# First block of a two-block network: attention bias added by VectorE from a stored band, a value group between the first heads, first branch's product beside the last heads

## The reference

```python
mod = (silu(c) @ w_mod + b_mod)                  # 6 x 1024, one row
h = rms_norm(x, norm_mix) * (1 + scale_m) + shift_m
qa, ka, va, xr, yr, qc, kc, vc, g_logits = split(h @ w_in)
# q and k are normalised by head of 64; 8 heads of branch a (window 128, a sink
# each), 8 heads of branch c; bias by distance q - k from a table per head
s = q @ k.T / 8 + bias[q - k]                    # causal
p = softmax(s)                                   # with the sink in branch a
o_a, o_c = p @ v
o_b = rg_lru(conv(xr)) * gelu(yr)
merged = g0 * (o_a @ wb[:512]) + g1 * (o_b @ wb[512:1536]) + g2 * (o_c @ wb[1536:])
x = x + gate_m * (merged @ w_out)                # g = sigmoid(g_logits)
```

## Time and profile before

| | us |
|---|---|
| median of 3 runs (2408.05 to 2409.7) | 2408.58 |
| the profiled execution | 2410.9 |
| its span, first to last instruction | 2409.2 |
| first dense matmul starts | 49.95 |
| end of the first value group | 170.5 |
| first g group starts | 208.93 |
| first branch_b group starts | 328.3 |
| w_out starts | 393.78 |

### The profile page before, as it was taken

How to read it: one execution, slowest core, us unless ns; L and a number is a source line. 1 busy time by engine, 2 the same in 40 slices (tenths; PEclk the granted TensorE clock), 3 DMA queues, 4 the chain that set the end, 5 groups by cost and what they waited for, 6 DMA issues and landing times.

```text
span 2409.2 us, 35095 instructions
## 1 busy us (share of the span) xinstructions
PE 2258.7 (94%) x14043; PEld 2032.7 (84%) x14043; DVE 1762.6 (73%) x1924; ACT 1324.5 (55%) x1277; POOL 53.0 (2%) x112
## 2 busy tenths in 40 slices
PE   7989998998998889999888699999999999999997
PEld 6987888998998879999888688888888888888886
DVE  5765756787598555547865388988888888888885
ACT  2563432663454444435344376767777776777674
POOL 5000000000000000000000000000000000000000
PEclk7997999999999999999999799999999999999998
DMA  8543754565743526665443299999999899999992
GB/s 260 175 153 115 226 162 145 154 186 178 205 154 108 158 78 187 182 181 165 127 140 125 71 375 329 370 342 354 369 332 373 321 374 338 366 326 366 332 382 108
DMA packets 414056, 565.70 MB, mean 235 GB/s; under 512 B 16330, under 2 KB 267444, under 8 KB 413904
## 3 DMA queue, kind: packets, MB, share of 16 engines
q1 hardware_dynamic: 410160, 556.31, 68.2%
q0 software_dynamic: 3456, 6.13, 1.2%
q10 hardware_dynamic: 288, 1.05, 0.1%
HBM read 562.37 MB, written 1.08 MB: 234 GB/s over the span
## 4 chain that ended last, share of the span: by engine, by line
PE 80%; DVE 9%; ACT 4%; issue 2%; DMA 0%; ACTq 0%; DVEq 0%
PE pair L1017 57%; PE misc L1017 13%; DVE arena L1882 2%; DVE wlo L1539 2%; PE misc L1412 1%; PE pair L1423 1%; ACT whi L594 1%; PE misc L1447 1%; PE misc L1196 1%; PE misc L1195 1%; PE misc L1080 1%; DVE rt L1564 1%; PE misc L1324 0%; DVE opl L1557 0%; DVE opf L1597 0%
## 5 line engine op out<-in xcount | busy, mean ns | idle before, releaser
L2078 DVE TENSOR_TENSOR wlo<-raw,whi 128x2048 fp32r<-128x2048 f32 x338 | 770.1, 2290 | 124.1 <-ACT whi L948 122.8
L948 ACT CAST whi<-raw 128x2048 fp32r<-128x2048 f32 x338 | 647.2, 1918 | 202.4 <-PE pair L1017 101.0
L1017 PE MATMUL pair<-hh,whi 128*128 128x256 f32 x1840 | 533.2, 290 | 28.0 <-DVE hl L1557 19.6
L1539 DVE TENSOR_TENSOR wlo<-raw,whi 128x2048 fp32r<-128x2048 f32 (+1 forms) x170 | 384.6, 2264 | 197.7 <-ACT whi L594 197.1
L1017 PE MATMUL pair<-hl,whi 128*128 128x256 f32 x1840 | 527.8, 287 | 0.0
L1017 PE MATMUL pair<-hh,wlo 128*128 128x256 f32 x1840 | 527.6, 287 | 0.0
L1017 PE MATMUL pair<-whi,oph 128*128 128x512 f32 (+1 forms) x1024 | 394.1, 385 | 5.3 <-DVE wlo L2078 3.6
L1017 PEld LDWEIGHTS pair<-hh,whi 128*128 128x128 f32 x1840 | 361.1, 196 | 33.7 <-issue 32.7
L1017 PE MATMUL pair<-wlo,oph 128*128 128x512 f32 (+1 forms) x1024 | 386.6, 378 | 0.0
L1017 PE MATMUL pair<-whi,opl 128*128 128x512 f32 (+1 forms) x1024 | 385.9, 377 | 0.0
L1017 PEld LDWEIGHTS pair<-hl,whi 128*128 128x128 f32 x1840 | 361.0, 196 | 0.3
(11 more groups left out here) (408 smaller groups left out, 2552.7 us busy)
## 6 DMA issues: line engine op xcount, KB each, us to landing
raw<-in_moe_w_gate_dram SPq DMA_DIRECT2D x114, 1024.0 KB, 7.3
raw<-in_moe_w_up_dram SPq DMA_DIRECT2D x112, 1024.0 KB, 7.3
raw<-in_moe_w_down_dram SPq DMA_DIRECT2D x112, 1024.0 KB, 6.9
raw<-in_w_in_dram SPq DMA_DIRECT2D x38, 1024.0 KB, 5.4
raw<-in_w_mod_dram SPq DMA_DIRECT2D x24, 1024.0 KB, 6.8
raw<-in_w_up_dram SPq DMA_DIRECT2D x44, 512.0 KB, 5.0
raw<-in_w_xkv_dram SPq DMA_DIRECT2D x16, 1024.0 KB, 5.6
raw<-in_ffn_w_gate_dram SPq DMA_DIRECT2D x22, 512.0 KB, 3.9
```

What stands on the lines that cost most here:

```text
L948: act.copy(whi[:, q, :], raw[:, r, :]).then_inc(sem("hi_ready"), 1)
L1017: ins = pe.matmul(out_, lhs, rhs, start=start and i == 0, stop=stop and i == 2)
L1539: dve.tensor_tensor(wlo[:, i_ % SPLIT, 0:size], raw[:, raw_of(n), 0:size], whi[:, i_ % SPLIT, 0:size].bitcast(F32), ALU.subtract).then_inc ...
L2078: dve.tensor_tensor(wlo[:, q, :], raw[:, r, :], whi[:, q, :].bitcast(F32), ALU.subtract).then_inc(sem("lo_ready"), 1)
```

## The change

- Bias: GpSimd stores each head's bias row 128 times, 384 wide, in DRAM (`bias_bands`), and loads it for a head with a row step of 383, so that partition q holds the bias of query q. `peak` becomes two `tensor_tensor_reduce` instructions: scores from PSUM plus band, written to SBUF, with the maximum as a second result. The bias matmuls and the flipped identity go. The exponentials read SBUF.
- Order at the start of attention: spreads and scores of the first heads come before the second value group, and VectorE's reciprocal no longer stands behind the splits of g slots.
- Branches: branch_a (half a slot) runs beside each of the last four heads, after branch_b; four groups branch_c of half a slot follow the heads; w_out's first group waits chunk by chunk.
- Start: of the first eight modulator slots PE takes 0, 2, 5 and 7, by products with one stationary column and 256 moving ones, a copy by ScalarE and a turn; slot 7 is loaded after xr's first slot. The tables for norms of q and k are made after the vector loads.
- Two places only change how a semaphore is named (feed-forward taps; `bc_done`).

```diff
-    modulator(8)
+    modulator(7)
     for j in range(4):
         dense("xr", w_in, [(XR + j * 256, 256)], "act")
+        modulator(j == 0)
...
         modulator(j == 0)
+        dense("branch_a", wb, [(j * 256, 256)], "dve", kchunks=4)
     for j in range(4):
-        parts = [(rows(wb, 0, 4), 0, 4, j * 256, 256, 0), (rows(wb, 12, 4), 4, 4, j * 256, 256, 0)]
-        groups.append(("branch_ac", [(parts, 8)], "dve"))
+        dense("branch_c", wb, [(j * 256, 256)], "dve", kchunks=4, k0=12)
...
+    bands = nc.dram_tensor("bias_bands", (NHEAD, P, BAND), F32).ap()
     mod_slots = [first_slot[g] for g in stage_groups["mod"]]
-    mod_on_pe = (0, 3, 6)
+    mod_on_pe = (0, 2, 5, 7)
     pe_no = {j: i for i, j in enumerate(mod_on_pe)}
-    dve_no = {j: i for i, j in enumerate(j for j in range(24) if j not in mod_on_pe)}
+    dve_mods = [j for j in range(24) if j not in mod_on_pe]
+    dve_no = {j: i for i, j in enumerate(dve_mods)}
+    column_no = {j: i for i, j in enumerate([1, 3, 4, 0, 2, 5, 6, 7, *range(8, 24)])}
...
             pool.memset(consts[:, 0:1], EPS).then_inc(sem("consts_ready"), 1)
...
             vector_loads()
+            link(pool.memset(hsel[:], 0.0))
...
+            link(pool.memset(spread[:], 1.0))
...
+            pool.memset(consts[:, 2:3], 0.0).then_inc(sem("tables_ready"), 1)
...
-            pool.dma_start(bias_dram, brow).then_inc(sem("brow_stored"), 16)
-            pool.wait_ge(sem("brow_stored"), 16)
+            pool.dma_start(bands, brow[:, 0:BAND].unsqueeze(1).to_broadcast([NHEAD, P, BAND])).then_inc(sem("bands_stored"), 16)
+            pool.wait_ge(sem("bands_stored"), 16)
 
...
             for h in range(NHEAD):
                 if h >= 2:
-                    pool.wait_ge(sem("att_scores"), h - 1)
-                pool.dma_start(bias_buf[h % 2], bass.AP(bias_dram.tensor, h * 512, [[1, P], [P, 2], [1, P]]))\
+                    pool.wait_ge(sem("att_max"), 2 * (h - 1))
+                pool.dma_start(bias_buf[h % 2], bass.AP(bands.tensor, h * P * BAND + P - 1, [[BAND - 1, P], [1, T]]))\
                     .then_inc(sem(f"bias_landed{h % 2}"), 16)
...
+            def row_copy(i):
+
+                act.wait_ge(sem("mod_direct"), i + 1)
+                act.copy(rows_of_mod[:, i, :], banks[0:1, i, 0:T]).then_inc(sem("mod_row"), 1)
+
+            row_copy(0)
+            row_copy(1)
             act.wait_ge(sem("squares_summed"), 1)
             act.activation(rt[:], misc[:, 0, 0:T], ACT.Sqrt, bias=consts[:, 0:1], scale=1.0 / D)\
                 .then_inc(sem("root_ready"), 1)
+            row_copy(2)
             ahead_of(stage_groups["xr"][0], 0)
+            row_copy(3)
             high("mix", shift=0)
             ahead_of(stage_groups["xr"][0], 2)
...
+            act.wait_ge(sem("bands_stored"), 16)
...
+            values_out(0)
             act.wait_ge(sem("rnn_ob_lo"), 2)
-            ahead_of(stage_groups["g"][0], 1)
             expo(0)
             for h in range(NHEAD):
                 if h + 1 < NHEAD:
                     expo(h + 1)
+                if h == 0:
+                    values_out(1)
                 turned(h)
                 if h % 2 == 0 and h >= 2:
                     out_high(h // 2 - 1)
-                ahead_of(beside[h])
+                ahead_of(beside[h], 2 if h < 12 else 3)
                 if 1 <= h <= 12:
                     gate(h - 1)
-            ahead_of(stage_groups["branch_ac"][0])
             out_high(7)
 
...
+            def mod_product(j):
+
+                n, i = mod_slots[j], pe_no[j]
+                pe.wait_ge(sem("x_copied"), i + 1)
                 pe.wait_ge(sem(f"landed{raw_of(n)}"), landed_at[n])
+                for c in range(DC):
+                    ins = pe.matmul(banks[0:1, i, 0:T], cact[:, c:c + 1], raw[:, raw_of(n), c * 256:(c + 1) * 256],
+                                    start=(c == 0), stop=(c == DC - 1))
+                ins.then_inc(sem("mod_direct"), 1)
+
+            def mod_turned(j):
+
+                pe.wait_ge(sem("mod_row"), pe_no[j] + 1)
                 for m in range(2):
+                    ins = pe.matmul(mod_bank(2 * j + m, 2 * j + m + 1), rows_of_mod[:, pe_no[j], m * P:(m + 1) * P], ones[0:1, 0:1],
+                                    start=True, stop=True)
+                ins.then_inc(sem("mod_columns"), 1)
 
...
-            mod_direct(0)
+            mod_product(0)
+            mod_product(2)
+            mod_columns(1)
             for j in range(4):
                 sums(0, j, start_sq)
+            mod_columns(3)
             pe.wait_ge(sem("vec0_landed"), 16 * N_VEC0_DMAS)
             pe.transpose(misc[:, 1, 0:P], stage_rows[:, 0, :], ident[:]).then_inc(sem("pe_start"), 1)
...
+            mod_product(5)
             mod_columns(4)
+            mod_turned(0)
+            mod_turned(2)
+            mod_turned(5)
+            mod_columns(6)
+            mod_product(7)
+            mod_turned(7)
...
             dense_group(stage_groups["vc"][0], hh, hl, weights_move=True)
-            pe.wait_ge(sem("qk_rs"), 1)
-            spread_roots(range(6))
-            dense_group(stage_groups["vc"][1], hh, hl, weights_move=True)
-            spread_roots(range(6, 14))
 
...
-                    pe.wait_ge(sem("att_exp"), exps(h - 2))
-                pe.wait_ge(sem(f"bias_landed{h % 2}"), 16 * (h // 2 + 1))
+                    pe.wait_ge(sem("att_max"), 2 * (h - 1))
+                pe.wait_ge(sem("qk_normed"), 6 if h < 8 else 14)
                 for i, (qb, kb) in enumerate(((0, 0), (1, 0), (1, 1))):
-                    s = misc[:, h % 2, i * P:(i + 1) * P]
-                    pe.matmul(s, q[:, qb * P:(qb + 1) * P], k[:, kb * P:(kb + 1) * P], start=True, stop=False)
-                    ins = pe.matmul(s, flip, bias_buf[h % 2][:, 1 - (qb - kb), :], start=False, stop=True)
+                    ins = pe.matmul(misc[:, h % 2, i * P:(i + 1) * P], q[:, qb * P:(qb + 1) * P], k[:, kb * P:(kb + 1) * P],
+                                    start=True, stop=True)
                 ins.then_inc(sem("att_scores"), 1)
 
-            pe.wait_ge(sem("qk_normed"), 14)
-            pe.wait_ge(sem("flip_ready"), 1)
-            pe.wait_ge(sem("act_read"), reads_at[stage_groups["vc"][1]])
+            pe.wait_ge(sem("qk_rs"), 1)
+            pe.wait_ge(sem("tables_ready"), 1)
+            spread_roots(range(6))
             scores(0)
             scores(1)
+            spread_roots(range(6, 10))
+            dense_group(stage_groups["vc"][1], hh, hl, weights_move=True)
+            spread_roots(range(10, 14))
+            pe.wait_ge(sem("qk_normed"), 14)
             for h in range(NHEAD):
                 pe.wait_ge(sem("att_p"), 2 * (h + 1))
...
                 if h < 12:
                     dense_group(beside[h], hh, hl)
                 else:
+                    pe.wait_ge(sem("rnn_ob_lo"), 2)
                     dense_group(beside[h], oph, opl, chunk0=4)
+                    pe.wait_ge(sem("att_out_lo"), 4)
+                    dense_group(stage_groups["branch_a"][h - 12], oph, opl)
                 pe.wait_ge(sem("att_pt_sb"), h + 1)
...
             pe.wait_ge(sem("att_out_lo"), 8)
...
+            for g in stage_groups["branch_c"]:
+                dense_group(g, oph, opl, chunk0=12)
...
-            for g in stage_groups["vc"]:
-                ahead_of(g)
+            ahead_of(stage_groups["vc"][0], 0)
 
...
+            def qk_norm(tiles):
+                for t in tiles:
+                    dve.wait_ge(sem("qk_spread"), t // 2 + 1)
+                    dve.scalar_tensor_tensor(qk[:, t], qk[:, t], col(names[t], 0), spread_bank(t), ALU.mult, ALU.mult)\
+                        .then_inc(sem("qk_normed"), 1)
 
             def peak(h):
                 b, s = h % 2, small[:, h % 2]
                 dve.wait_ge(sem("att_scores"), h + 1)
+                dve.wait_ge(sem(f"bias_landed{h % 2}"), 16 * (h // 2 + 1))
                 if h >= 2:
-                    dve.wait_ge(sem("att_p"), 2 * (h - 1))
-                dve.tensor_reduce(s[:, 0:1], misc[:, b, 0:P], AX_X, ALU.max).then_inc(sem("att_max"), 1)
-                dve.tensor_reduce(s[:, 1:2], misc[:, b, P:384], AX_X, ALU.max).then_inc(sem("att_max"), 1)
+                    dve.wait_ge(sem("att_pt"), h - 1)
+                floor = sinks[:, h:h + 1] if h < 8 else NEG
+                dve.tensor_tensor_reduce(s_buf[b][:, 0:P], misc[:, b, 0:P], bias_buf[b][:, P:T], 1.0, floor, ALU.add, ALU.max,
+                                         s[:, 0:1]).then_inc(sem("att_max"), 1)
+                dve.tensor_tensor_reduce(s_buf[b][:, P:384], misc[:, b, P:384], bias_buf[b], 1.0, floor, ALU.add, ALU.max,
+                                         s[:, 1:2]).then_inc(sem("att_max"), 1)
                 dve.wait_ge(sem("att_max"), 2 * h + 2)
-                if h < 8:
-                    dve.tensor_scalar(s[:, 2:4], s[:, 0:2], sinks[:, h:h + 1], -1.0, ALU.max, ALU.mult).then_inc(sem("att_negmax"), 1)
-                else:
```

(44 more changed lines are left out.)

132 lines of the change are left out of this document (41 added, 91 removed).

## The result

The changed kernel takes 2385.77 us (median of 4 runs, 2381.81 to 2388.86) against 2408.76 for the kernel before in the same comparison: ratio 0.9903, 95% interval 0.9886 to 0.9921. It is faster by 23 us where 39 were forecast, and 2385.8 lies above the range of 2357 to 2384. The profiled execution took 2386.11 us with a span of 2384.4.

The account below looks back on a forecast made before the run. The prediction took TensorE, busy 94% of the span, as the bound. Its terms 3 + 15 + 16 + 5 = 39 us took the profiled 2410.9 to 2371.9, less 2.3 to the median: 2370 us, range 2357 to 2384.

Parts of the forecast that it names:

- The step that failed: Storing the 3.1 MB of bias bands: 14 us at 225 GB/s under 52 us of cover, so no cost.
- one of 16 engines' pace: Rival, chance 0.05: band store at 18.5 GB/s takes 170 us, ScalarE waits about 118 us past its cover; 2488 us.
- Start: Modulator products at the kernel's start: 0.7 us gained at slow clock, 5.3 at fast; 3 us taken.
- V to G: From vc's first value group to the first g group: reordered spreads, scores and reciprocal save 16.8 us, taken as 16.
- the forecast case: Main case, chance 0.50, 2370 us: the clock falls after the value group as in the old trace.
- Twelve heads: Heads' loop: dropping three bias products cuts a head from 9.86 to 8.61 us, PE still the bound; 15 us saved.
- the +0.45 taken: Extra VectorE us per head for fused add and maximum; lower bound the reduces' own price, upper bound +1.27.
- Last heads and branches: Last four heads and branch products, b0 to w_out: 60.2 us in place of 65.5, saving 5 us.
- The stall ahead of a0: In head 12, PE waits once for a ScalarE cast and tanh before the first branch_a product; 1.8 us.
- The clock around the value group: Rival, chance 0.15: clock stays up there and in the start, giving 2363 us, down to 2360.
- VectorE as the bound: Rival, chance 0.15: fused instruction costs +1 us or more a head in the loop; 2377.5 to 2379 us at +1.27.
- tail and start: Rival, chance 0.12: both give nothing, as slot 7 lands late and the c loop waits; 2378 us.

Follow-up runs that it names:

- small_store: Changed kernel storing only the 16 bias rows (32 KB) instead of the 3.1 MB of bands, so bias values are not the reference's; 2372.91 us, 0.9851 of before.
- paced_store: Changed kernel with its band store from SBUF cut into eight pieces, one behind each step of the recurrence's convolution; 2375.43 us, 0.9851 of before.
- dd_bands: Changed kernel storing the 16 rows, then copying each head's band from its row, DRAM to DRAM, in 0.2 MB pieces; 2371.79 us, 0.9853 of before.
- recip_first: Kernel before, with only VectorE's reciprocal of the q and k roots moved ahead of its casts for vc's second group and later slots; 2400.38 us, 0.9965.
- gate_first: Changed kernel with ScalarE's last gate tanh ahead of the cast for the slot three ahead, from the first two branch products' head; 2382.52 us, 0.9891 of before.

## Why the prediction was wrong

The step that failed is "At 225 GB/s it takes 14 us, so it costs nothing; weight loads share the engines with it at a share near 0.56 and have four slots of room." Three things in it were wrong. The store takes 34.2 us, not 14. The engines' time is the resource: the store took 28.9 us of all engines within its 34.2, a share of 0.85, beside loads that used 0.76 in the same part of the old trace (60.0 to 93.4 us). While the store lasts, 59.2 to 93.4, the engines' share is 1.00 and they move 142 GB/s, where the old trace has 222. And the four slots of room weren't there: the slot that ScalarE asked for at 80.1 had been sent for only at 67.5, as a slot comes free when VectorE has split it, so its room was 12.5 us against a landing of 28.7. The only wait that the prediction priced, ScalarE's before the decay, was indeed covered; the rival "one of 16 engines' pace" was about that wait too. I asked who waits for the store and not who waits beside it. small_store and the store in the kernel before put its price at 13 to 15 us in that stretch, and paced_store shows that the lump is what costs, since the same bytes from the same source in pieces hold no weights up. dd_bands has all of it back, and its 2371.8 us are inside the range and 2 from the forecast.

The other terms were of the right kind and most were a little low. They are taken from two profiles of each kernel, so that the clock's luck counts less, each as the difference of the two means in the table:

- Start, forecast 3: 45.4 against 43.8, 1.6. The first pair alone said 4. The forecast took one start, 47.86, for the rule; old starts lie between 42.9 and 47.9. Its price of the old direct form, 6.83 us "bound by loading 32 weight tiles", was one of two levels: in the second profile of the kernel before the same 32 products take 3.86 us. The new form takes 3.61 to 5.80 us in the changed kernel's two profiles; two such rows stand below.
- V to G, forecast 16: 37.6 against 19.8, 17.8. What carried it most is the reciprocal (37.6 to 28.2 in recip_first); the group's place is worth 1 to 2 (21.3 to 19.8). The 7 us between the two runs are left for the two heads' scores without bias products, the split norm and a softmax beside other work, which no run took apart. The clock fell as in the forecast case: 0.82 over the stretch, the group at 7.13 us.
- Twelve heads, forecast 15: 119.65 against 101.7, 17.9. The period is 8.43 us, not 8.61: the three bias products were priced at their sixth of 2.50 us each, 0.417, but a score product costs 0.29 when no bias product stands beside it, so 1.46 go, not 1.25. VectorE never became the bound. The fused pair costs +0.14 us in a head with a sink and +0.02 in the others, below the +0.45 taken, near the lower bound; no wait of PE for VectorE shows in 100.8 us. Its wait at the output's low half is 3.9 us over four times in 205 to 300 us, up to 1.3, where 0.4 was expected. The DMA engines' share in this stretch is 0.79, not 0.87.
- Last heads and branches, forecast 5: 65.5 against 59.8, 5.7. The stall ahead of a0, forecast 1.8, is 1.73, and gate_first removes it. The recorded terms of a head in this part add to 10.3 us where the sum uses 9.9; 9.9 is what the new trace has for two of them. B to N, which adds the first product's wait for the merged tiles, gives 6.2.
- N to L, forecast nothing: 1974.75 against 1979.2, so -4.45, by the luck of the clock in these four executions.
- M to V, forecast nothing: 122.6 against 136.65, -14.05.

Sum: 1.6 + 17.8 + 17.9 + 6.2 - 4.4 - 14.0 = 25.1, and the four profiled times give it: (2410.9 + 2405.0)/2 - (2386.1 + 2379.8)/2 = 25.0. The medians say 23. The terms that were forecast come to 43.5 us for 39, so without the store's collision the time would have been inside the range, as dd_bands shows.

PE's timeline at the start of the kernel before, second profile (the first is the earlier trace rows):

```profile
12.12 3.86 PE L1072 MATMUL misc<-cact,raw 128*128 128x1 f32 x32
15.84 5.15 PE L1080 MATMUL misc<-arena,ones 128*128 128x256 f32 x16
```

and the changed kernel:

```profile
10.48 3.61 PE L1080 MATMUL pair<-raw,cact 128*1 128x256 f32 x16 [0.81 <-DMA raw<-in_w_mod_dram]
17.56 4.92 PE L1080 MATMUL pair<-raw,cact 128*1 128x256 f32 x16 [3.46 <-DMA raw<-in_w_mod_dram]
```

The prediction read the earlier trace rows as "one-column products did not bring the fast clock". The second profile has the same products at 3.86 us, so the step from one profile to a rule was wrong. The clock column doesn't help here: it reads 1.00 in 12 to 19 us of the first profile, where they take 6.83. The Trainium skill, TensorE: Matmul & The Clock Gate, Part 1, says that activity releases the throttle. The new products agree with it so far as they go: sixteen take 3.61 us at a granted clock of 1.00, and 4.92 at 0.73 behind a pause of 3.46 us. The starts of the kernel before, slow in one execution and fast in another with the same work, neither confirm nor refute it.

The rivals. The clock around the value group fell as in the forecast case. VectorE as the bound did not come, tail and start gave about their terms, and the store's rival had the right object and the wrong victim. The Trainium skill's rule on two non-bf16 SBUF sources (Vector Engine (DVE) Microarchitecture Reference, Points that are easy to get wrong) speaks of another form than the fused one, which has one source in PSUM. No run here has the fused form with both sources in SBUF; for the plain form the row that the prediction read, 485 ns against 479, disagrees with it. The fused form's 0.48 us for 256 elements is the price of L1597.

Two things are still open: why the store in the kernel before costs 9 us more than its stretch shows, and why a store that repeats rows of 16 SBUF partitions moves 92 GB/s. That its price goes by bytes rests on two sizes; whether the number of partitions sets it was not tried.

## What to carry to other kernels

Price a background transfer by what the other queues lose: add its share of the engines' time to theirs over its own duration (0.85 and 0.76 here), and if that is above one, the loads beside it are late, whoever waits for the transfer itself. Read the loads' room from the trace, as the time from issue to need, and not from the number of buffers. Cut the transfer into pieces behind steps of the work (worth 10 us here), or make it from a small source in DRAM close to its use (14 us). And look for one short instruction that stands behind long look-ahead work on its engine: the reciprocal, moved ahead of two splits, gave 8 to 10 us by itself.

## What the runs showed of the hardware

- One DMA of 3.1 MB from 16 partitions of SBUF, each row repeated 128 times, moves 92 GB/s, takes 34 us, and stretches the landing of 1 MB loads on another queue from 6.0 to 29.4 us. It took 28.9 us of all 16 engines; the same bytes in eight spaced pieces took 20. Copies DRAM to DRAM of 0.2 MB took 3.8 us of all engines for 1.02 MB, 270 GB/s.
- An addition with a maximum as second result (128 x 256, one source in PSUM) takes 0.48 us and 0.08 for its accumulator's read, and the next instruction starts 0.52 us after it began.
- Two executions of one program differ by 8 us in 1980 through the clock at two places: over all profiles, 213.6 to 214.0 or 217.1 to 217.9 us from the norm ahead of the feed-forward part to the next one, and 78.8 to 78.9 or 81.4 to 82.8 in the cross attention. A single pair of profiles can't tell a loss of 8 us in unchanged code from this.
